# Modulation rows of a two-part transformer made on TensorE's column tiles during the attentions, and more of the expert rows summed on VectorE

## The reference, cut to what matters

```python
c_act = silu(c)
for l in range(2):
    mod = c_act @ w_ada[l] + b_ada[l]          # w_ada[l] is 1024 x 6144, 25 MB
    sh_m, sc_m, gt_m, sh_f, sc_f, gt_f = split(mod, 6)
    h = rms_norm(x, g_pre_mix[l]) * (1 + sc_m) + sh_m
    x = x + gt_m * rms_norm(token_mixer(h, w_in[l], ...), g_post_mix[l])
    h = rms_norm(x, g_pre_ffn[l]) * (1 + sc_f) + sh_f
    x = x + gt_f * rms_norm(conv_glu_ffn(h, ...), g_post_ffn[l])
```

## Time and profile before

| | us |
|---|---|
| median of 3 runs | 3621.55 (3619.16 to 3630.48) |
| the profiled execution | 3621.2 |
| its span in the trace | 3619.9 |
| TensorE busy / VectorE busy | 2892.3 / 2313.7 |
| data read from memory | 1105.58 MB, 306 GB/s over the span |

### The profile page before, as it was taken

One profiled execution on the slowest core, in us unless ns is written; L12 is line 12 of the kernel. 1 busy time (PEld: TensorE's weight loads), 2 busy tenths in 40 slices (PEclk: granted clock), 3 DMA queues, 4 the chain that ended last, 5 costly groups with the idle time before them and its releaser, 6 DMA issues.

```text
span 3619.9 us, 30466 instructions
## 1 busy us (share of the span) xinstructions
PE 2892.3 (80%) x9297; PEld 1538.4 (42%) x9297; DVE 2313.7 (64%) x4862; ACT 1136.4 (31%) x2905; POOL 981.6 (27%) x841
## 2 busy tenths in 40 slices
PE   5688967679988768987778777798779788777776
PEld 1344446356533336834446333343354463332222
DVE  0556538789867667875764998544423459975544
ACT  1112122323322352313451444333323224443333
POOL 0000000222332223332321444444310015443332
PEclk8789978689999889998879999899998889999999
DMA  8555732689979758997864999899962259999997
GB/s 333 173 191 204 248 123 94 227 343 363 358 288 409 273 205 323 417 408 262 315 242 157 392 421 421 347 420 421 421 238 75 70 211 419 421 421 421 422 421 332
DMA packets 214564, 1108.80 MB, mean 306 GB/s; under 512 B 24948, under 2 KB 25408, under 8 KB 116096
## 3 DMA queue, kind: packets, MB, share of 16 engines
q0 software_dynamic: 114512, 818.87, 56.1%
q1 hardware_dynamic: 99040, 287.27, 21.9%
q10 hardware_dynamic: 848, 0.72, 0.1%
HBM read 1105.58 MB, written 1.05 MB: 306 GB/s over the span
## 4 chain that ended last, share of the span: by engine, by line
PE 31%; DMA 29%; DVE 28%; ACT 4%; issue 4%; SPq 1%; POOL 1%; ACTq 0%; DVEq 0%; POOLq 0%
DMA AR<-in_uv,AR 24%; PE PS L805 9%; DVE AR L2244 7%; PE PS L2175 5%; PE PS L2088 3%; DMA AR<-in_w_in 2%; DVE AR L371 2%; PE PS L1127 2%; PE PS L1602 2%; DVE AR L2239 2%; PE PS L2186 2%; PE PS L787 1%; PE PS L2326 1%; DMA AR<-in_even_w_in 1%; DVE AR L1975 1%
## 5 line engine op out<-in xcount | busy, mean ns | idle before, releaser
L2294 POOL DMA_INDIRECT AR<-in_uv,AR x768 | 909.2, 1184 | 1577.9 <-PE PS L2175 641.3
L2244 DVE CUSTOM_DVE_ANT_0 AR<-AR 128x1024 f32<-128x1024 f32 x768 | 937.1, 1222 | 505.3 <-DMA AR<-in_uv,AR 503.2
L2175 PE MATMUL PS<-AR 128*128 128x512 f32 x2048 | 971.0, 622 | 288.6 <-ACT AR L2231 282.7
L2175 PEld LDWEIGHTS PS<-AR 128*128 128x128 f32 x2048 | 386.0, 196 | 867.1 <-ACT AR L2231 453.4
L805 PE MATMUL PS<-AR 128*128 128x512 f32 (+3 forms) x1080 | 470.5, 587 | 46.2 <-DMA AR<-in_w_in 20.8
L2213 ACT ACTIVATE AR<-AR 128x2 f32<-128x2 f32 x384 | 78.1, 203 | 1143.3 <-DVE AR L2244 1142.2
L1114 PE MATMUL PS<-AR 128*128 128x256 f32 x1408 | 322.1, 388 | 15.8 <-DMA AR<-in_w_up_lin 11.6
L805 PEld LDWEIGHTS PS<-AR 128*128 128x128 f32 x1080 | 204.1, 203 | 292.7 <-issue 241.7
L1114 PEld LDWEIGHTS PS<-AR 128*128 128x128 f32 x1408 | 269.9, 194 | 79.3 <-issue 19.7
L371 DVE SCALAR_TENSOR_TENSOR AR<-AR,CC 128x512 f32<-128x512 f32 x280 | 212.7, 760 | 67.5 <-DMA AR<-in_w_ada 44.6
L2231 ACT ACTIVATE AR<-C,AR 128x128 f32<-128x128 f32 (+1 forms) x614 | 241.0, 392 | 20.2
(11 more groups left out here) (235 smaller groups left out, 2652.4 us busy)
## 6 DMA issues: line engine op xcount, KB each, us to landing
AR<-in_w_ada SPq DMA_DIRECT2D x160, 256.0 KB, 8.1
AR<-in_w_in SPq DMA_DIRECT2D x56, 512.0 KB
AR<-in_w_mod SPq DMA_DIRECT2D x96, 256.0 KB, 4.5
AR<-in_peer_w_q SPq DMA_DIRECT2D x48, 512.0 KB
AR<-in_w_mod SPq DMA_DIRECT2D x45, 512.0 KB, 12.6
AR<-in_w_up_act SPq DMA_DIRECT2D x44, 512.0 KB
AR<-in_w_up_lin SPq DMA_DIRECT2D x44, 512.0 KB
AR<-in_w_down SPq DMA_DIRECT2D x44, 512.0 KB
```

What stands on the lines that cost most here:

```text
L2175: ins = pe.eng.matmul(acc[i][hh], e.dg(x), e.buf(x)[:, 1024 + 512 * hh:1536 + 512 * hh], start=(x == e.on[False][i][0]), stop=(x == e.on[F ...
L2244: v.eng.tensor_tensor_reduce(e.buf(x)[:, 0:1024], e.buf(x)[:, 0:1024], norm2(e).H[e.tiles[x // 128]], 1.0, 0.0, ALU.mult, ALU.add, DT[x // ...
L2294: g.eng.indirect_dma_start(e.buf(x), None, D["uv"][e.l], bass.IndirectOffsetOnAxis(ap=idx_at(x // 16, x % 16, 1), axis=0)).then_inc(*land. ...
```

## The change

It does seven things.
1. `ada0a` becomes `OneMods`, a `PairMods` whose stationary is `CP1` (the latent column broadcast to 32). It is made before the four steps ahead, and `cmods` is armed only after them. x and ctx are issued in the middle of the weights; the small loads move to GpSimd's queue.
2. The other rows 2 to 5 of both layers and 1, 0 of layer 1 are summed by a new class, `Quads`: four halves at a time, one in each column group of one bank; 3 quads in the attention of layer 0, 2 in that of layer 1. A step has 4 pieces of 256 KB and 4 products; a quad has 8 steps. The result is kept as four rows in `BR`.
3. `KeptAda` spreads kept rows over the partitions: `ada0b` and `ada1b` (now with row 2) in `wout`, `ada1a` in `up`.
4. `attended` does one step of the quads in each stage of the attention, two in the first five of layer 1; the context's queries do one in each of theirs.
5. The fills in the input projection and their guards on the norm's transposes are gone.
6. The quads' loads of layer l wait for its index scores (`sco`), since their five slots lie in areas in use until then.
7. `UPDOWN` gains rows 24 to 79.

```diff
+        OWN_Q = [MODt[:, 2048 + 512 * i:2560 + 512 * i] for i in range(3)] + [T[:, 3072 + 512 * i:3584 + 512 * i] for i in range(2)]
...
+        class Quads:
...
+            def sp(self, sp):
+                n = len(OWN_Q)
+                for q, (r0, halves) in enumerate(self.quads):
+                    for kc in range(8):
+                        for g, (l, r) in enumerate(halves):
+                            i = self.piece(q, kc, g)
+                            sp.wait_ge(("quad", self.key, i - n) if i >= n else self.guard)
+                            sp.eng.dma_start(OWN_Q[i % n], D["w_ada"][l][r, kc // 2, :, 512 * (kc % 2):512 * (kc % 2) + 512]).then_inc(
+                                *land.landed(f"quad{i % n}", "raw", self.key, i))
+                        yield
+                yield
+            def pe(self, pe):
...
+                    bk = bank(pe, SIDE, "quad", self.key, q)
...
+                            pe.wait_ge(("raw", self.key, i))
+                            pe.eng.matmul(bk[32 * g:32 * g + 32, :], CC[:, kc:kc + 1].to_broadcast([128, 32]), OWN_Q[i % n],
+                                          start=(kc == 0), stop=False).then_inc(*pe.done("quad", self.key, i))
...
+        class KeptAda(KeptMods):
...
+                pe.wait_ge(self.made)
+                pe.eng.matmul(bk, ident[96:128, r:r + 1].to_broadcast([32, 128]), BR[96:128, :], start=True,
+                              stop=True).then_inc(*pe.done("mm", "mod", self.key, j, hh, 0))
...
-        CH, ROW, PACE, ATT = 0.45, 0.47, 0.6, (1.2, 0.5)
+        CH, ROW, PACE, ATT, QUICK = 0.45, 0.47, 0.6, (1.2, 0.5), (0, 5)
...
+        def attended(lane, l, steps):
+
+            for i, _ in enumerate(steps):
+                lane.fill(1 + (i < QUICK[l]), "q")
+                yield ATT[l]
...
-            pe.run(mods_of["first", l])
...
-                if i >= 4 * len(HEAD[l]):
-                    pe.fill()
-                yield CH
-            pe.flush()
...
+            pe.flush("c")
+            pe.run(mods_of["quads", l], "q")
+            pe.fill(1, "q")
             yield 1.0
...
-            for _ in stages(8, s1, s2, s3):
-                yield ATT[l]
+            yield from attended(pe, l, stages(8, s1, s2, s3))
+            pe.flush("q")
+            pe.run(mods_of["first", l])
...
+                pe.fill(2)
+                yield CH
+            pe.flush()
             pe.run(mods_of["next", l])
...
-        ATTENTION, UPDOWN = range(108, 122), range(131, 195)
+        ATTENTION, UPDOWN = range(108, 122), (*range(24, 80), *range(131, 195))
...
+        start = mods_of["start"] = OneMods("ada0a", D["w_ada"][0], 0, [
+            (1, 1, "scale", D["g_pre_mix"][0]), (0, 0, "shift", None)], FIRST[0],
+            [("pair", "mod0c1", *mods_of["c", 1].halves[2][:2], 3)], WIDE_L, mods_of["c", 1].finished())
...
+                quads = mods_of["quads", 0] = Quads("early", [(112, [(0, r) for r in (4, 5, 8, 9)]), (116, [(0, r) for r in (6, 7, 10, 11)]),
+                                                              (120, [(1, r) for r in (2, 3, 0, 1)])],
+                                                    [("sco", 0, 1)] + mods_of["c", 1].finished(), [])
...
+                quads = mods_of["quads", 1] = Quads("later", [(124, [(1, r) for r in (4, 5, 8, 9)]), (112, [(1, r) for r in (6, 7, 10, 11)])],
+                                                    quads.summed() + [("sco", 1, 1), ("added", 0, 2), ("added", 0, 3)],
+                                                    [("mm", "mod", "ada0b", j, hh, 0) for j in (2, 4) for hh in range(2)] + [("added", 0, 3)])
...
-            lane.run(cmods, "c")
             lane.run(Ready(keep1, keep2), "keep")
             for i, share in enumerate(even(lane, "c")):
+                if i == AHEAD - 1:
+                    lane.run(cmods, "c")
...
             for share in queries(lane, of_ctx):
+                lane.fill(1, "q")
                 yield PACE * share
...
-            if lane.name == "sp":
-                rows(lane)
+            rows(lane)
             for _ in range(AHEAD):
                 next(beside)
```

More of the change, by code:

```diff
@@ L277, in __init__ @@
                 self.own, self.named, self.wide = own, "own", wide
-                self.ring = SIDE if not wide else FIRST[0] if accs else EARLY
+                self.ring = SIDE
                 self.key, self.row0, self.jobs, self.accs = key, row0, jobs, accs
@@ L441, in __init__ @@
                 self.count = len(self.halves) + 1
+                self.columns, self.older = CP, self.guard
+                if wide:
+                    self.ring = EARLY
             def finished(self):
@@ L530, in dve, with __init__, finished @@
                 return self.each(v, lambda *_: None, self.out_dve)
+        class OneMods(PairMods):
+            def __init__(self, key, w, row0, jobs, ring, guard, wide, older):
+                PairMods.__init__(self, key, w, row0, jobs, {}, guard, wide)
+                self.columns, self.ring, self.older = CP1, ring, older
+            def finished(self):
+                return [("mm", "mod", self.key, j, hh, 0) for j, hh, outs in self.halves[-2:]]
         class KeepMods(Mods):
@@ L916, in start_act, with second_rows_act @@
             first_rows(a)
+        def second_rows_act(a):
+            rows = mods_of["start"].steps(a)
+            next(rows)
+            next(rows)
+            next(rows)
+            norm_of["f", 0, 1].squares(a, ("pair", "ada0a", *mods_of["start"].halves[0][:2], 0))
+            through(rows)
         def start_dve(v):
@@ L977, in ada_rows @@
                     4: (1, "scale", D["g_pre_ffn"][l]), 3: (0, "shift", None), 5: (3, "gate", D["g_post_ffn"][l])}[j]
-        def ada(key, l, js, accs, frees, guard=(), own=(), wide=()):
-            return Mods(key, D["w_ada"][l], 12 * l, [(j, [(0, *ada_rows(j, l))]) for j in js], accs, frees, guard,
-                        own=own, wide=wide)
         def rope(v, x1, x2, c, s, r):
@@ L1187, in first_pool @@
                     *land.landed(f"go{i}", "go", l, i))
+            g.flush("c")
+            g.run(mods_of["quads", l], "q")
+            g.fill(1, "q")
             yield 1.0
-            for _ in range(10):
-                yield ATT[l]
+            yield from attended(g, l, range(10))
+            g.flush("q")
+            g.run(mods_of["first", l])
             yield 1.0
             for _ in lin(g, 8, (0, 1024), [0, 1], nothing):
+                g.fill(2)
                 yield CH
+            g.flush()
             add_pool(g, l, 2, ("mix", l))
@@ L1298, in s2 @@
                                  ("mm", "av", l, u - 2) if u >= 2 else None).then_inc(*a.done("ev", "pt", l, u, kt))
-            for _ in stages(8, s1, s2, nothing):
-                yield ATT[l]
+            yield from attended(a, l, stages(8, s1, s2, nothing))
+            a.flush("q")
+            a.run(mods_of["first", l])
             for t in range(2):
@@ L1477, in s3 @@
                 v.events["ev", "av", l, u] = v.last
-            for _ in stages(8, s1, s2, s3):
-                yield ATT[l]
+            yield from attended(v, l, stages(8, s1, s2, s3))
+            v.flush("q")
+            v.run(mods_of["first", l])
             rs = []
@@ L1494, in first_dve @@
             for _ in lin(v, 8, (0, 1024), [0, 1], nothing):
+                v.fill(2)
                 yield CH
-            add_dve(v, l, 2, ("lin", "wout", l), mods_of["first", 0] if l == 0 else mods_of["next", 0])
+            v.flush()
+            add_dve(v, l, 2, ("lin", "wout", l), mods_of["first", l])
             v.run(mods_of["next", l])
```

208 lines of the change are left out of this document (132 added, 76 removed).

## The result

The changed kernel takes 3647.15 us (median of 6 runs, 3640.79 to 3653.93), the kernel before 3621.41 in the same session (6 runs, 3612.43 to 3630.48). The ratio is **1.0066**, 95% interval 1.0053 to 1.0078: slower by 26 us, where 3572 was forecast in a range that ended at 3630. The profiled execution took 3648.3 us for a span of 3646.8.

What follows compares the result with a forecast made beforehand. No single engine bounds the whole (TensorE 80% busy, VectorE 64%), each stage having its own limit. Stage terms -48.5 - 6 + 17 + 8 - 15 - 8 - 21 + 24 = -49.5 gave 3572 us, range 3515 to 3630.

Steps and rivals of the forecast that it cites:

- Part 1: Start: VectorE's sums go to TensorE, first product of the projection at 86 us instead of 134.5; minus 48.5.
- Part 2: Input projection of layer 0: sums and waits leave, four context halves add 28 us; minus 6 (plus 10 to minus 20).
- Part 3: Attention of layer 0: 25 quad steps fit in, some 12 wait 2.4 us, 5 for `sco`; plus 17 (0 to 50).
- Part 4: `wout` of both layers: 8 spreads each, about 0.87 us, through one bank; plus 4 each (0 to 7).
- Part 5: Up of layer 0: VectorE loses 34.5 us, gains 28.3, bounds at 97% full; minus 15 (0 to minus 25).
- Part 6: Down of layer 0: TensorE loses 10.9 us, stage takes 81; minus 8 (3 to 10).
- Part 7: Projection of layer 1: six halves go, memory and TensorE 110 us each, together 120; minus 21 (15 to 30).
- Part 8: Attention of layer 1: 16 quad steps, five pairs waiting for landings among gathers; plus 24 (0 to 60).
- first rival: Attentions: TensorE waits for quad pieces, 2.2 us a step decides; costs of 151 us give 3682; chance 0.12.
- the attentions did not swallow it: Rival in both attentions: the quad work costs only 5 us in each, giving 3541; chance 0.2.
- VectorE did give back in the feed-forward: Rival in up and down of layer 0: no gain, 42 us of sums against 34.5 removed; 3595; chance 0.15.
- changes of tile shape: Rival in the quad steps: 41 steps with two 0.7 us TensorE stops each, 57 us, giving 3629; chance 0.05.

Runs made afterwards that it cites:

- no landings: Changed kernel with only each layer's first five quad pieces loaded, all products kept; 3572.87 us, ratio 0.986 against the kernel before.
- one block of eight: Changed kernel with only the first of each quad's eight steps loaded and multiplied; 3560.02 us, ratio 0.9823 against the kernel before.
- Early spreads: The nine slots kernel with the first four of eight halves of kept rows spread right after the attention; 3575.53 us, ratio 0.9871 against the kernel before.
- nine slots: Changed kernel with nine ring slots instead of five, seven pieces issued before the index scores; 3580.26 us, ratio 0.988 against the kernel before.

## Why the prediction was wrong

- **Part 1, start: right.** Forecast 86 for the first product of the projection, measured 84.3. TensorE's sums keep pace with landing and the four context halves do leave the start.
- **Part 2, projection of layer 0: too small a gain** (-17.6 for -6, within its bounds). The term that was too large is the 28 for the four halves that came in: TensorE's busy time fell by 8.7 us (313.0 to 304.3) though 18.6 of sums went out, so they brought it some 10 us and not 22, and its idle time fell from 63.7 to 54.8.
- **Part 3, attention of layer 0: this step failed**, +68.5 for +17 and outside its bounds of 0 to 50. It counted the right loop (a ring of one step and one piece) and mis-sized the products in it. It took a step's products at 1.02 us, from a row in which all blocks had landed, 26 in all, and let them fit beside the other work at no cost. In single file they are busy 62.5 us, and 32.4 with the landings away; the forecast has the difference nowhere. Two thirds of the products is hidden when they run together, not all. The waits were counted fairly: 12 of 2.4 us forecast, 29 in all, and 5 for the head; in TensorE's timeline 12 of the 23 steps behind the first have a wait for a landing, and all such waits come to 21.7 us beside the head's 13.2. Most of them did take the place of idle time, as forecast, though idle time still grew by 12.5 us. Of the 68.5 us the landings are 41.9 ("no landings"), the rest of the products 8.6 ("one block of eight"), and 18.0 are open. Of the two waits that show there, the one at the head was not taken away in any run, and the one for ScalarE's copy only changed sides. So whether 5 us was right for the head is open too.
- **Part 4, `wout`: failed in size**, +35.3 in both layers for +8. The spreads are two records each, 1.12 us, not 0.87: 16 of them, 18 us, where 14 were counted and partly hidden. In layer 0 nothing hides them: from 683.43 to 725 TensorE has no idle time, its busy time grows by 7.8 us and the stage by 11.5. In layer 1 (+23.8) an order that was priced at nothing comes on top. The end of the stage in TensorE's timeline, and VectorE's copies of the same spreads; line 887 is `wout`'s own second half, one tile of 128 tokens after the other:

```profile
1371.49 8.40 PE L887 MATMUL PS<-AR 128*128 128x512 f32 x16
1379.82 1.12 PE L704 MATMUL PS<-BR,C 32*128 32x512 f32 x2
1380.87 7.13 PE L887 MATMUL PS<-AR 128*128 128x512 f32 x16
1387.94 1.12 PE L704 MATMUL PS<-BR,C 32*128 32x512 f32 x2
```

```profile
1381.04 0.69 DVE L380 TENSOR_TENSOR MOD<-PS,MOD 128x512 f32<-128x512 f32 x1 [8.97 <-PE PS L704]
1389.16 0.69 DVE L380 TENSOR_TENSOR MOD<-PS,MOD 128x512 f32<-128x512 f32 x1 [7.44 <-PE PS L704]
```

  The last two spreads stand behind these products in TensorE's order, and VectorE, in order too, waits for them before it comes to the residual sum of the first tile. That sum needs neither the last spread nor the second tile's products: ScalarE has the factor of its norm at 1381.3, and VectorE comes to it at 1391.2. In the kernel before, it was made while TensorE still worked on the second tile. That this order makes the 23.8 us is read from the timeline; no run changes it alone. "Early spreads", which has four spreads ahead of `wout`, has the stage 14.0 us shorter in this layer and keeps it so, and in layer 0 gives back most of what it gains. A second bank for the spreads was not tried.
- **Part 5, up: right in its sum (-14.3 for -15)**, and in its reason, VectorE as the bound. It counted 22 further sums where there are 17, and took 97% busy where it is 91%; the two errors cancel. The experiments add what the forecast should have said: the sums in this stage lose 19 us of the 33 that the move of the modulation gives.
- **Part 6, down: right** (-6.9 for -8).
- **Part 7, projection of layer 1: -36.1 for -21**, past its bound of 30. It expected memory and TensorE to bound together, 120 us where each alone would take 110. But without the six halves TensorE waits for memory no more: between the same marks the DMA share falls only from 0.89 to 0.84, yet of the 15.9 us that TensorE waited for `w_in` none is left, and from 1074 to 1173 it runs without a gap. TensorE's group of the projection, before and after:

```profile
L805 PE MATMUL PS<-AR 128*128 128x512 f32 (+1 forms) x224 | 94.3, 571 | 17.1 <-DMA AR<-in_w_in 15.9 <-ACT AR L861 1.0
```

```profile
L905 PE MATMUL PS<-AR 128*128 128x512 f32 (+1 forms) x224 | 89.1, 552 | 1.0 <-ACT AR L961 1.0
```

- **Part 8, attention of layer 1: failed in size**, +50.5 for +24, inside its bounds of 0 to 60. By the same loop: 35.3 us of it are the landings (line 665 is busy 46.6 us, and 23.3 with the landings away), 4.7 the rest of the products, 10.5 are open.

The forecast's first rival, given 0.12, is what happened: 2.2 us of path a quad step was its point of decision, and the attentions grew by 119 us over 40 steps, 3.0 a step (192 and 128 records of line 665, eight to a step; the forecast had 41). Its price of 151 us was too high, and the larger gains of parts 2 and 7, less what `wout` cost, kept the total at +26 instead of +61. The other rivals: the attentions did not swallow it; VectorE did give back in the feed-forward; the start moved; changes of tile shape do not stop TensorE for 0.7 us (in the kernel without landings the 64x128 product starts 0.54 us after the narrow ones of 480.99 start, which themselves start 0.46 after those before them).

On the one rule that was weighed, the Trainium skill (DMA: Bandwidth & Descriptors, "Anatomy of one DMA") gives an estimate of 2.6 us for a piece of 256 KB, by which part 3 would have come out at about zero; the forecast took the trace's 4.1. The page gives its fit for DMAs that GpSimd issues, and the 3.6 to 4.6 us of the trace are loads of GpSimd too, so there the measurement decides. The pieces go through SyncE's queue. Their landing stands in no view, but where TensorE waited for a piece its product starts with the landing. The first and the fourth piece of layer 0, issued at 473.40 and 474.72, are multiplied at 477.08 and 481.56, 3.7 and 6.8 us later:

```profile
473.40 1.28 SPq L651 DMA_DIRECT2D MOD<-in_w_ada  x3
474.72 0.92 SPq L651 DMA_DIRECT2D AR<-in_w_ada  x2
```

Both are beyond 2.6 us. But what was missing in the forecast was not the length of one landing.

## What to carry to other kernels

Where an in-order engine frees the slots from which its own next loads are issued, count the ring in steps, not in pieces: a ring that holds one step and one piece made half of the steps wait for a landing, and a ring of two steps and a piece, filled earlier (nine slots here), is worth 67 us of 3647. Before products are priced by a row, ask whether their data had landed in that row: singly they cost up to four times as much. Idle time can take up waits, as most of these, and still the stage grows if busy time is added to them. When an experiment is to take a wait away, look in its trace whether the wait is gone. And a shift of work that pays where one engine bounds (the sums in down, 5 to 7.5 us gained) costs where the other does (in up, 19 lost); price it by stage.

## What the runs showed that was not expected

- Four 128x32 by 128x512 products in four column groups take 1.07 us if their pieces have all landed, and about 1.04 us each if they come singly. With no product added, line 665 was busy 62.5 us instead of 32.4 in the attention of layer 0, and 46.6 instead of 23.3 in that of layer 1.
- The granted clock rose in the attentions, to 0.89 from 0.75 in layer 0 and to 0.82 from 0.75 in layer 1, and TensorE's other products in the first took 82 us instead of 92; the stage still grew. In up the clock fell from 0.93 to 0.88 when the sums left TensorE, and to 0.85 where VectorE had 241 us of work. TensorE's busy share alone does not give it: without landings TensorE is busy 77% of the first attention at 0.82, in the changed kernel 73% at 0.89.
